# Two transformer blocks in float32: one expert matrix loaded beside the weight ring

## The reference

```python
def expert_choice_ffn(h, router, w_gate, w_up, w_down):
    cap = CAPACITY_FACTOR * t // N_EXPERTS          # 32 tokens for each expert
    aff = softmax(h @ router)
    gate, idx = lax.top_k(swapaxes(aff, 1, 2), cap)
    xs = h[bidx, idx]
    hid = silu(einsum('becd,edf->becf', xs, w_gate)) * einsum('becd,edf->becf', xs, w_up)
    y = einsum('becf,efd->becd', hid, w_down) * gate[..., None]
    return zeros_like(h).at[bidx, idx].add(y)
```

## Time and profile before

| | us |
|---|---|
| median of 3 runs | 2728.86 (2728.52 to 2733.14) |
| the profiled execution | 2730.3 |
| its span in the trace | 2728.3 |
| PE busy | 2356.9 (86%) |
| DVE busy | 583.0 (21%) |
| ACT busy | 373.3 (14%) |
| DMA over the span | 239 GB/s mean, 651.93 MB |

### The profile page before, as it was taken

How to read it: one execution, slowest core, us unless ns; L and a number is a source line. 1 busy time by engine, 2 the same in 40 slices (tenths; PEclk the granted TensorE clock), 3 DMA queues, 4 the chain that set the end, 5 groups by cost and what they waited for, 6 DMA issues and landing times.

```text
span 2728.3 us, 39444 instructions
## 1 busy us (share of the span) xinstructions
PE 2356.9 (86%) x17780; PEld 1541.6 (57%) x17780; DVE 583.0 (21%) x1235; ACT 373.3 (14%) x851; POOL 30.9 (1%) x56
## 2 busy tenths in 40 slices
PE   8999999989999999899989897888799876656564
PEld 6788688477886884445545554554454543323222
DVE  1201100023011000534443121222311441101112
ACT  1211000012210000215433000000102320000000
POOL 0000000000000000000000000000000000000000
PEclk9999999999999999999989999999999988888878
DMA  8444675353436774300042999999920068999997
GB/s 297 151 137 145 235 269 209 130 210 133 151 123 232 262 249 139 133 0 1 1 185 95 426 425 427 426 426 426 386 81 0 0 247 357 427 428 426 428 427 303
DMA packets 165387, 651.93 MB, mean 239 GB/s; under 512 B 8039, under 2 KB 55523, under 8 KB 140515
## 3 DMA queue, kind: packets, MB, share of 16 engines
q1 hardware_dynamic: 161392, 639.66, 60.0%
q0 software_dynamic: 3312, 8.79, 1.0%
q10 hardware_dynamic: 514, 0.94, 0.1%
HBM read 648.27 MB, written 1.08 MB: 238 GB/s over the span
## 4 chain that ended last, share of the span: by engine, by line
PE 54%; issue 28%; DMA 13%; DVE 3%; ACT 1%; DVEq 0%; ACTq 0%; POOL 0%; POOLq 0%
PE psum L1962 11%; DMA ring<-in_moe_w_up 10%; PE psum L1817 8%; PE psum L1894 6%; PE psum L1977 5%; PE psum L438 4%; PE psum L1882 3%; PE psum L631 3%; PE psum L562 2%; PE psum L430 2%; DMA ring<-in_moe_w_gate 2%; PE psum L1944 1%; PE psum L1795 1%; PE psum L1843 1%; DMA ring<-in_moe_w_down 1%
## 5 line engine op out<-in xcount | busy, mean ns | idle before, releaser
L631 PE MATMUL psum<-ring,arena 128*32 128x256 f32 x6144 | 402.2, 417 | 177.1 <-DMA ring<-in_moe_w_up 94.9
L631 PEld LDWEIGHTS psum<-ring,arena 128*32 128x32 f32 x6144 | 216.7, 118 | 359.6 <-issue 153.5
L1962 PE MATMUL psum<-ht,ring 128*128 128x256 f32 x1408 | 310.8, 382 | 2.1 <-ACT ht L2017 2.1
L1962 PEld LDWEIGHTS psum<-ht,ring 128*128 128x128 f32 x1408 | 266.9, 191 | 41.8 <-issue 5.7
L648 PE MATMUL psum<-ring,lnp 128*32 128x256 f32 x3072 | 195.6, 409 | 77.3 <-DMA ring<-in_moe_w_down 73.7
L648 PEld LDWEIGHTS psum<-ring,lnp 128*32 128x32 f32 x3072 | 106.5, 116 | 165.2 <-issue 56.0
L438 PE MATMUL psum<-ring,ht 128*128 128x512 f32 x448 | 194.9, 594 | 0.0
L1894 PE MATMUL psum<-ht,ring 128*128 128x256 f32 x768 | 166.7, 379 | 0.0
L1894 PEld LDWEIGHTS psum<-ht,ring 128*128 128x128 f32 x768 | 145.9, 190 | 20.7 <-issue 1.0
L1977 PE MATMUL psum<-ring,arena 128*128 128x512 f32 x352 | 151.5, 593 | 2.3 <-DVE arena L2237 2.3
L1387 DVE TENSOR_TENSOR arena<-psum,arena 32x512 f32<-32x512 f32 (+1 forms) x128 | 70.8, 553 | 386.0 <-PE psum L648 384.7
(11 more groups left out here) (336 smaller groups left out, 1934.3 us busy)
## 6 DMA issues: line engine op xcount, KB each, us to landing
ring<-in_moe_w_gate SPq DMA_DIRECT2D x64, 2048.0 KB
ring<-in_moe_w_up SPq DMA_DIRECT2D x64, 2048.0 KB
ring<-in_moe_w_down SPq DMA_DIRECT2D x64, 2048.0 KB
ring<-in_w_in SPq DMA_DIRECT2D x52, 1024.0 KB
ring<-in_ada_w SPq DMA_DIRECT2D x48, 1024.0 KB
ring<-in_w_ffn_gate SPq DMA_DIRECT2D x22, 1024.0 KB
ring<-in_w_ffn_up SPq DMA_DIRECT2D x22, 1024.0 KB
ring<-in_w_ffn_down SPq DMA_DIRECT2D x20, 1024.0 KB
```

The lines of the kernel that those rows point to most:

```text
L631: last = mm(bank[32 * j:32 * j + 32, SPLIT * m:SPLIT * m + SPLIT], x_four[:, k, e % 4, SLOTS * m:SLOTS * m + SLOTS], slot[:, k % 4, SPLIT ...
L1962: last = mm(bank[:, SEQ * u:SEQ * u + SEQ], slot[:, k, SEQ * u + P * h:SEQ * u + P * h + P], xT[:, k, :], start=k == 0, stop=k == KT - 1)
```

## The change

It does four things.

- The up matrix of expert 1 (`besides`) no longer goes through the ring. SP loads it behind g0, u0 and y0 and ahead of g1: it waits for the event of `("lgT",)` of the mixer, then issues its first half (2 MB) into `arena[4096:8192]`, and its second half as two DMAs of 1 MB into `ht[2048:4096]` and `arena[14336:16384]`. PE's `up` waits for `side_in` instead of a panel and reads the rows from there. `TICK` keeps PE's event for the first half without a panel. The ring thus carries 94 instead of 96 panels in each loop.
- The places that become occupied are cleared: `gb_moe` gets a tile of its own, `y_four` moves to `arena[2048:4096]`, `sil_e` to where the index blocks were, and `sel_T`, `sel_m` and `sel` into the selection's area.
- DVE makes `spread_back` (`ways_back`) behind `hidden(1)`, once PE has read the up matrix out of `ht`.
- `dec` names its ring slot by the panel number, since the numbers shift by two.

```diff
@@ -41,7 +41,7 @@
-    REL, EV = "rel", "ev"
+    REL, EV, TICK = "rel", "ev", "tick"
 
     def __init__(self):
         self.events, self.panels = 0, 0
@@ -57,6 +57,8 @@
             elif e == self.EV:
                 ev += 1
                 pan.append(ev)
+            elif e == self.TICK:
+                ev += 1
             else:
                 ev += 1
                 b = n % BANKS
@@ -229,6 +231,11 @@
     return steps + [("c", GROUPS - 1)]
 
 
+def besides(kind, e):
+
+    return (kind, e) == ("u", 1)
+
+
 def plan_moe(banks, layer):
     R, EV = BankPlan.REL, BankPlan.EV
     src = streams_of(layer)
@@ -238,7 +245,9 @@
     banks.plan(f"moe{layer}", moe)
     order = []
     for kind, e in expert_steps():
-        if kind in "guy":
+        if kind in "guy" and besides(kind, e):
+            order += [BankPlan.TICK, (kind, e)]
+        elif kind in "guy":
             order += [EV, (kind, e), R]
         elif kind == "r":
             order += [("rep",)]
@@ -298,9 +307,10 @@
 
     xh = view(arena[:, 8192:12288], 4, D)
     x_four = view(arena[:, 0:2048], KT, 4, 64)
-    gb_moe = view(arena[:, 2048:4096], STREAMS, D)
-    y_four = view(arena[:, 4096:6144], STREAMS, D)
-    sil_e = view(arena[:, 6144:7168], 2, HALF)
+    gb_moe = sb("gb_moe", [P, STREAMS, D])
+    y_four = view(arena[:, 2048:4096], STREAMS, D)
+    side = [[view(arena[:, 4096:8192], 4, D)],
+            [view(ht[:, 2048:4096], 2, D), view(arena[:, 14336:16384], 2, D)]]
     pick = view(ht[:, 0:2048], STREAMS, TT, GROUPS, P)
     spread_back = view(ht[:, 2048:4096], STREAMS, GROUPS, SEQ)
     hid_e, hidT = view(lflat[:, 0:1024], 2, HALF), view(lflat[:, 1024:2048], 2, HALF)
@@ -313,10 +323,11 @@
     block_0 = view(arena[0:64, s0 + 1024:s0 + 1280], STREAMS, P)
     block_r = view(arena[0:64, s0 + 1280:s0 + 2048], STREAMS, 3 * P)
     logit_T = arena[:, s0 + 1024:s0 + 1152]
+    sil_e = view(arena[:, s0 + 1024:s0 + 2048], 2, HALF)
     rT = view(arena[:, 4096:8192], KT, 2 * SEQ)
-    sel_T = arena[0:32, s0 + 2048:s0 + 2176]
-    sel_m = view(arena[:, s0 + 2176:s0 + 2208], STREAMS, GROUPS, 4)
-    sel = view(arena[:, s0 + 2240:s0 + 2256], 2, STREAMS, GROUPS)
+    sel_T = arena[0:32, s0 + 864:s0 + 992]
+    sel_m = view(arena[:, s0 + 992:s0 + 1024], STREAMS, GROUPS, 4)
+    sel = view(arena[:, s0 + 200:s0 + 216], 2, STREAMS, GROUPS)
 
     qT, kT = view(arena[:, 0:2048], HEADS, SEQ), view(arena[:, 2048:6144], HEADS, 2 * SEQ)
     rv, rg = view(arena[:, 6144:10240], 4, D), view(arena[:, 10240:12288], TT, D)
@@ -324,7 +335,7 @@
     gaps = view(arena[:, 12288:14848], 5, HALF)
     rope_t = view(arena[:, 14848:15360], 2, SEQ)
     rot_a, rot_b = arena[:, 15360:15872], arena[:, 15872:16384]
-    dec = view(ring[:, 4, :], 2, 4, HALF)
+    dec = view(ring[:, (banks.stage_panels["mix1"][0] + 2) % RING, :], 2, 4, HALF)
     ry = c[:, :, :]
     ryT = view(arena[:, 2048:4096], KT, SEQ)
     rsq = view(arena[:, 15360:15872], TT, 2, DV)
@@ -341,6 +352,7 @@
              "kt_ready", "final_ready", "inv_ready", "half_ready", "tile_squares", "tile_ms", "tile_rms", "tile_inv",
              "tile_xh", "rtc_ready")
     Q = {n: sem(n) for n in names}
+    side_in = [sem(f"side_in_{h}") for h in range(2)]
 
 
     def sync(sp, load_panel):
@@ -356,10 +368,18 @@
 
         def experts(layer):
             w = {k: I[f"moe_w_{m}_2"][layer] for k, m in (("g", "gate"), ("u", "up"), ("y", "down"))}
-            for kind, e in expert_steps():
-                if kind not in w:
+            matrices = [(kind, e) for kind, e in expert_steps() if kind in w]
+            held = [m for m in matrices if besides(*m)]
+            rest = [m for m in matrices if not besides(*m)]
+            for kind, e in rest[:3] + held + rest[3:]:
+                rows = w[kind][e].rearrange("(p j) n -> p j n", p=P)
+                if besides(kind, e):
+                    sp.wait_ge(pe_done, banks.full(f"mix{layer}", ("lgT",)))
+                    for h in range(2):
+                        r = 4 // len(side[h])
+                        for i, part in enumerate(side[h]):
+                            sp.dma_start(part, rows[:, 4 * h + r * i:4 * h + r * i + r, :]).then_inc(side_in[h], 8 * r)
                     continue
-                rows = w[kind][e].rearrange("(p j) n -> p j n", p=P)
                 for h in range(2):
                     first, _, _ = banks.release[n[0] - RING]
                     sp.wait_ge(pe_done, first)
@@ -620,17 +640,21 @@
                 bank = open_bank(pe, stage, (kind, e))
                 for k in range(KT):
                     if k % 4 == 0:
-                        slot = panel(0, D)
+                        if besides(kind, e):
+                            pe.wait_ge(side_in[k // 4], 32 * (layer + 1))
+                        else:
+                            slot = panel(0, D)
                         if kind == "g" and e % 4 == 0:
                             if e:
                                 gathered(stage, ("x", e // 4), k // 4)
                             else:
                                 gathered(f"moe{layer}", ("x",), k // 4)
+                    row = (side[0][0][:, k, :] if k < 4 else side[1][k // 2 - 2][:, k % 2, :]) if besides(kind, e) else slot[:, k % 4, :]
                     for m in range(n):
                         for j in range(4):
                             last = mm(bank[32 * j:32 * j + 32, SPLIT * m:SPLIT * m + SPLIT],
                                       x_four[:, k, e % 4, SLOTS * m:SLOTS * m + SLOTS],
-                                      slot[:, k % 4, SPLIT * j:SPLIT * j + SPLIT],
+                                      row[:, SPLIT * j:SPLIT * j + SPLIT],
                                       start=k == 0 and m == 0, stop=k == KT - 1 and m == n - 1)
                     if k % 4 == 3:
                         last.then_inc(pe_done, 1)
@@ -1355,12 +1379,14 @@
                     wait_emptied(dve, stage, ("rep",))
                 else:
                     step(ins)
-            for s in src:
-                for g in range(GROUPS):
-                    ins = TS(spread_back[:, s, g, :], iota, sel[:, 0, s, g:g + 1], sel[:, 1, s, g:g + 1], ALU.is_equal,
-                             ALU.mult)
-            step(ins)
-            V.memset(spot(0), 0.0).then_inc(Q["back_ready"], 1)
+            def ways_back():
+
+                for s in src:
+                    for g in range(GROUPS):
+                        ins = TS(spread_back[:, s, g, :], iota, sel[:, 0, s, g:g + 1], sel[:, 1, s, g:g + 1], ALU.is_equal,
+                                 ALU.mult)
+                step(ins)
+                V.memset(spot(0), 0.0).then_inc(Q["back_ready"], 1)
 
             width = SPLIT * len(src)
 
@@ -1404,6 +1430,8 @@
             for kind, e in expert_steps():
                 if kind == "u":
                     hidden(e)
+                    if besides(kind, e):
+                        ways_back()
                 elif kind == "y":
                     weighted(e)
                 elif kind == "x":
```

## The result

The changed kernel takes **2713.78 us** (median of 5 runs, 2713.35 to 2714.42), the kernel before in the same comparison 2728.86 us (5 runs, 2728.52 to 2733.14). The ratio is 0.994 with a 95% interval of 0.9928 to 0.9952: 15.1 us faster where 19.65 were forecast. The time lies in the range, 4.6 us above the predicted 2709.2. The profiled span is 2711.8 us, 16.5 less than before.

The account below looks back on a forecast made before the run. Bytes over 427 GB/s in the two expert loops were taken to bound the kernel. The span of 2728.3 less 19.65 us, with all other terms 0, gave 2709.2 us against the median; range 2706.5 to 2716.0.

Parts of the forecast that it names:

- What bounds the kernel: In both expert loops, bytes over 427 GB/s set the end; around them runs a chain of PE, DVE and ACT steps.
- Part 1: One matrix of 4.194 MB leaves each layer's stream: 9.85 us gained in layer 0, 9.80 in layer 1, 19.65 together.
- Part 2: The matrix is loaded in the idle gap ahead of gate 1, with 5 to 12 us to spare: cost 0.
- Part 3: The stream still never pauses; tightest at gate 3 in layer 0, lead 1.75 us: pause 0, other end 1.5 us.
- Part 4: Layer 0's eight DVE instructions (2.67 us) moved behind expert 1's hidden rows, plus moved views and semaphores: 0.
- The sum: Whole kernel: span 2728.3 - 19.65 = 2708.65 us, 2710.65 as a run, 2709.2 against the median.
- A: Whole kernel as summed: 2709.2 us, or 2710.7 with the one pause; own range 2707.5 to 2711.5; chance 0.71.
- B: The ring runs dry in layer 0, giving back part or all of its 9.85 us: 2711.5 to 2719.0; chance 0.11.
- C: A late panel, layer 0's last matrix, also goes away, 1.5 to 3 us less: 2706 to 2707.5; chance 0.05.
- D: A wait elsewhere ends both loops when they end now: 2728.9 us, unchanged; chance 0.07.
- E: The new load's SBUF writes slow DVE and ACT in the selection: about 2733 or 2741 us; chance 0.06.
- The sign: Whole kernel faster, meaning below 2723.4 us, as a measurement can tell about 0.2%, 5.5 us; chance 0.87.

Follow-up runs that it names:

- y1_again: Repetition of y1_beside, the changed kernel with expert 1's down matrix instead of its up matrix beside the ring: 2711.23 us, ratio 0.9935.
- y1_beside: Changed kernel with expert 1's down matrix instead of its up matrix beside the ring, way-back matrices moved behind expert 1's weighted rows: 2709.93 us, ratio 0.9923.
- y1: y1_beside and y1_again together, the changed kernel with expert 1's down matrix beside the ring: 2709.93 and 2711.23 us.
- layout_only: Changed kernel with its buffers and way-back matrices moved, but every matrix through the ring in both layers: 2731.32 us, ratio 1.0003 to the kernel before.
- before: The kernel before the change, unchanged, in its first profile: 2728.86 us median, span 2728.3 us.
- before_again: The kernel before, unchanged, run for a second profile: 2730.53 us, ratio 0.9999.
- after: The changed kernel in its first profile: 2713.78 us, ratio 0.994 to the kernel before.
- after_again: The changed kernel, unaltered, run for a second profile: 2713.0 us, ratio 0.9932 to the kernel before.
- no_side_load: Changed kernel without the side loads and their waits, expert 1's share of the output left wrong: 2712.51 us, ratio 0.9931 to the kernel before.
- layer0_only: Changed kernel with the side load in layer 0 alone, buffers and way-back matrices as in the change: 2721.31 us, ratio 0.9968 to the kernel before.
- layer1_only: Changed kernel with the side load in layer 1 alone, buffers and way-back matrices as in the change: 2722.07 us, ratio 0.9967 to the kernel before.
- side_in_stream: Changed kernel with its side loads issued behind gate 1 instead of ahead of it, same bytes and places: 2730.71 us, ratio 0.9995 to the kernel before.

## Why the prediction came out as it did

- **What bounds the kernel** was right. Shortening each stream by one matrix shortened each by one matrix's time, to within 0.8 us.
- **Part 1**, forecast 9.85 and 9.80 us. Layer 1 gave 9.8 (447.6 as the mean of five traces with the whole layer in the stream, 437.8 of five without the matrix; y1_again stands apart with 439.3: the last two windows of 1 us of its stream moved 33 and 16 GB/s, where y1_beside has one such window, so with 427 / 16 = 27 GB/s for a DMA engine, an estimate, one engine or two came in late). Layer 0 gave 9.75 where the pause is away (y1), 9.1 with it. The 358 GB/s that the Trainium skill states ("DMA: Bandwidth & Descriptors", Specifications) would have asked for 23.4 us together; the streams still ran at 426 to 428 GB/s and the gain did not reach that.
- **Part 2**, cost 0, was right, and the estimates of its end were too: forecast 1481.5 to 1486, measured 1483.7; in layer 1 2251.3 to 2256, which with gate 1 8.3 us sooner is 2243.0 to 2247.7, measured 2244.2.
- **Part 3** is the one step of mechanism that failed, by a small size. The lead was as worked out: by 1530 the stream had moved 14.37 MB (152, 428, 429 and 428 GB/s in the four windows of 10 us), the other 2.41 of the eight panels last until 1535.6, and gate 3 is issued at 1533.93, 1.7 us for a forecast 1.75. But 1.7 us do not cover the start of a load as the 1.5 us of ramp had it; DMA dipped and lost 0.6 to 0.8 us. The ramp was read from the bytes moved after an issue out of idle, which tells what a start costs in bytes, not how early the next load must be queued for no dip. The second end of the part, 1.5 us, held it.
- **Part 4** and the layout: 0, right (layout_only, 1.0003). `ways_back` takes DVE 2.64 us at 1532.21, behind expert 1's `hidden`, which had waited 11.03 us for PE; DVE then waits 9.32 us more for PE.
- **The sum.** Against 2728.86 it gave 15.1 us, against the medians of the later jobs 17.6 (2730.58 - 2713.0). So some 2 us of the missing 4.6 are the starting point: five runs of a kernel whose runs spread over 10 us had a median 1.9 us lower than 25 runs. 0.6 us is the pause. 1.7 us is a term that the sum did not have: the last combine, which took 3.70 us at full clock in before, before_again and layout_only, takes 5.40 in after, after_again, no_side_load, layer0_only, layer1_only and y1_beside. 1.9 + 0.6 + 1.7 = 4.2 of 4.6; of these the first is a difference of medians (few runs, or another chip: not separated), the other two were read from single profiled executions. The two executions of the stage table can be booked without a rest, and give the same picture: 1.44 because the one profiled before lay above its median (2730.3 against 2728.86), 1.08 ahead of gate 1, 0.46 in layer 0's stream, -0.20 in layer 1's, 0.00 between them, 1.81 at the end, together 4.6.
- **The clock in the last combine** is a term that the sum put at nothing without a word. The work is the same; 5.40 for 3.70 us is the granted clock, 0.69 and 1.00. Whether the change makes the fall likelier is open. One kernel shows both values, 5.40 in y1_beside and 3.70 in y1_again, so it is not fixed by the change. But of the eight traces with 94 ring panels in at least one loop seven show 5.40, and the three with 96 in both show 3.70.
- **From last load to next mixer** the stage took 61.55, 58.68, 58.07, 57.66, 56.02 and 55.95 us where layer 0's stream is shorter (after, after_again, no_side_load, layer0_only, y1_beside, y1_again) and 55.9 to 59.3 where it isn't. Two things make up most of the difference: the down product starts 26.2 to 27.8 us behind the issue of its load, and the combine takes 7.13 to 10.19 us, by the clock. In layer0_only, with 7.13, it is the late start (27.78): the down matrix of expert 14 was read 6.5 us behind the panel ahead of it instead of 5.0, and all later panels 1.5 us late with it, though no window of 1 us between 1900 and 1920 moved less than 377 GB/s. Why stays open.
- **The rivals.** A is what happened, with the one pause; its own range (to 2711.5) missed the measured median by 2.3 us, since it took in no error of the starting point and no change of clock. B's mechanism, a dip near 1535, is there, but costs 0.6 us instead of up to 10. C did not come in the profiled execution: PE still waits 2.70 us for layer 0's last down matrix. D falls with side_in_stream and the streams' lengths. E falls with 24.43 against 24.41 us. The sign and the bound of 0.2% held.

## What to carry to other kernels

Where a ring feeds a stream that sets the time, look for the stretches in which the ring is full and idle, and for buffers outside it that nobody needs just then: a load moved there is worth its bytes over the stream's rate and nothing more, and the same buffers filled during the stream are worth nothing. Choose the matrix by the ring, too: the one that leaves must not pull a load up to a release that comes late (here the down matrix instead of the up matrix spares the one dip). And take more than three or five runs of the kernel before as the base of a forecast of half a per cent, for its own scatter may be as large as the error.

## What the runs showed of the hardware

- **The clock behind short waits.** Behind an idle stretch of 2.91 or 2.92 us TensorE ran the same 16 matmuls partly at the 0.5 grant (1.2 GHz) in three traces and wholly at full clock in eight: 7.13 us, or 8.56, 8.69 and 10.19. The last 8 took 3.70 or 5.40 us behind 1.83 to 1.86. One kernel showed 10.19 and 8.56 in two executions, another 5.40 and 3.70. Up to 3.1 + 1.7 = 4.8 us of a 2712 us kernel hang on these two places.
- **Float32 matmuls of 128 x 512** with 128 columns of weights show as two records each, and take 0.90 us at full clock (5.42 us for six).
- **The queue's lead.** A load of 2 MB that was issued 1.7 us before the queued ones ended left a dip of 0.6 to 0.8 us; 2.9 us of lead, at gate 2 of the kernel before, left none.
- **The end of a stream.** The last 4 us of layer 1's stream moved about half the rate, in the kernel before and in the changed one: from 2703 to 2707 us 197 to 229 GB/s in the first, from 2685 to 2689 197 to 246 in the second. The end of a stream is therefore not bytes over 427 GB/s; it is the same in both, so it drops out of a difference.
- **Loads beside compute.** 382 to 394 GB/s into SBUF cost DVE, ACT and PE nothing that shows: 24.43 against 24.41 us for the selection in layer 0, and 21.51 (after_again) against 21.55 and 21.54 (the kernel before) in layer 1.
